# Norm factors and rows of maxima spread over the partitions by DMA through a scratch in memory, instead of by transposes on TensorE

## The chip, the cores and the metric

The kernel runs on one core of one Trainium2 chip. The metric is the device time of one execution in microseconds: 1445.86 us before the change (median of three runs, 1445.59 to 1446.18). All arithmetic is in float32; the large products are made of three TensorE products of numbers split into a high and a low part.

## The reference

The input x has 512 positions of 1024 features. Three blocks work on it one after the other:

```
block 1:  h = rms(x, norm_w) @ w_in                       # 1024 -> 3584 columns
          qa, ka = rms over 64 features of each (head, half), 4 heads x 2 halves
          oa = rms over 128 of (softmax(q0 k0) - lam * softmax(q1 k1)) @ va, per head
          orr = rms over 128 of retention (forward + backward), 4 heads
          x += [oa * silu(ga), orr * silu(gr)] @ w_out
block 2:  mLSTM, 4 heads: gates i, f in both directions; b = cumsum(log_sigmoid(f));
          M = running maximum of (i - b);  weights exp(i - b - M) * (q k), summed over keys,
          divided by max(|sum|, exp(-m));  rms over 256, * sigmoid gate;  x += .. @ m_out
          x += swiglu(rms(x))
block 3:  windowed attention with rope and a sink;  x += .. @ a_out;  x += swiglu(rms(x))
          return rms(x)
```

Two things in it matter here. The rms of queries, keys and head outputs gives one factor for each position (and for each half of a head). The running maximum M of mLSTM is one row of 512 numbers for each head and direction. The kernel keeps features on partitions and positions along the free axis, so each of these rows must be present on all partitions before it can be multiplied or added.

## The kernel before, in words

All activations lie as tiles of 128 features by 512 positions. A weight chunk is 128 x 2048 numbers (1 MB). It is loaded by SyncE's queue into one of two buffers RAW (`w_load`, L352), split by ScalarE into a high part WH and by VectorE into a low part WL (`split`, L299, with `copy`, whose instruction is recorded at L216, and `tt`, L229), and used by TensorE in 48 matmuls: 8 k-tiles, 2 output tiles, 3 products each (`mm3`, L268, recorded at L261). The load of chunk j+2 is put into SyncE's queue when the last part of chunk j has been given to the splitting engines.

The order of the instructions on every engine is written by a planner while the program is built. Each engine has a `Queue` with a model time `t`; each result has a model time in `WHEN`. `weave` (L124) takes pieces of two streams: the main stream (projections, then the output projection) and the side stream (attention, retention or mLSTM heads), and a list `soon` of short steps that are issued when the inputs are due by the model. If the side stream's next piece is due at TensorE's model time it goes first; else the main stream goes on. A stream that finds its input not made gives up its turn. Every engine executes its queue strictly in the planned order and waits on semaphores, so an instruction whose input is late holds all that stands behind it on that engine.

Four pools of buffers are handed out oldest first: 8 banks of PSUM (`bank`), 25 tiles of split operands (`fr`), 12 temporary tiles of 128 x 512 (`ft`), and small columns (`sc`).

Block 1 projects 14 chunks in the order a0 a1 q0 g0 q1 g1 q2 q3 v0 v1 r0 r1 g2 g3. Each q chunk gives a query tile and a key tile of one head. For both, `qk_norm1` copies and squares the tile, `qk_norm2` sums the squares over 64 features with four small matmuls on TensorE (the result is a column of 8 numbers on each of the 128 partitions, one for each of 4 groups of positions and 2 halves), takes the power -1/2 on GpSimd (`rpow`) and multiplies with the block's own norm factor. It then widens the 8 columns to 128 x 512 on VectorE (L754), and `qk_norm3` transposes this with four transposes of 128 x 128 (`spread`, L474, recorded at L293) into a bank of PSUM, from where VectorE multiplies it into the tile. The side stream `diff_heads` works on head hd as soon as the query and key of that head are split; there are 16 items of head and query tile.

The outputs of the heads go through `head_norm`, `head_col` (four small matmuls, a power) and `head_spread` (four transposes, one product on VectorE). Heads 0 to 3 are those of the attention (head 3 is finished in the next side stream, `ret_heads`), 4 to 7 those of the retention. `ret_heads` begins when the four tiles of chunks r0 and r1 are split.

In block 2 `m_gates` computes the gates of all heads with scans on VectorE. The negated maxima NM lie as rows 0 to 3 (forward) and 32 to 35 (backward) of a tile of 64 x 512. Four transposes bring them into 256 columns `ncol`; eight more do the same for two other quantities, `acol` and `ecol`, which the change leaves. For each head, `rows` makes two tiles of 128 x 512 from `ncol` with four transposes and a copy by ScalarE each (L1442 to L1444). `part` then adds a column to such a tile, takes the exponential and multiplies with the product of query and key; the four parts of a head are put into the queues right behind `rows`, without a wait of the planner for the rows. `outp` multiplies with the values. Head hd can start when the main stream has projected its query and key.

`load` (L308) is the helper for single DMAs. The rope step of block 3 (`halves`, L1631) already moves tiles of 32 x 512 from SBUF to SBUF with four DMAs each, which is the only such use before.

Of the kernel before, what the change touches and what calls it, by code (L numbers as in the profile page):

```python
# [5 lines left out]
ALU = mybir.AluOpType  # L6
ACT = mybir.ActivationFunctionType
F32 = mybir.dt.float32
# [4 lines left out]
S = 512  # L13
# [35 lines left out]
WHEN = {}  # L49
# [112 lines left out]
def blocks_kernel(nc, A, out):  # L162
# [64 lines left out]
    def tt(o, a, b, op, *after, q=DV):  # L227
        us = dve_us(o) if q is DV else 0.95
        return q.op(lambda e: e.tensor_tensor(o, a, b, op), *after, us=us)  # L229
# [494 lines left out]

    GS2 = CO[:, K_GS:K_GS + 2]

    def qk_norm1(b, t):

        f, ff = ft.take()
        q, qf = ft.take()  # L730
        t1 = copy(FT[:, f, :], PS[:, b, :], t, ff)
        t2 = act(FT[:, q, :], PS[:, b, :], ACT.Square, t, qf)
        bank.put(b, t1, t2)
        return f, t1, q, t2

    def qk_norm2(got, w):
        f, t1, q, t2 = got
        b, fb = bank.take()
        for i in range(4):
            t = mm(PS[:, b, 2 * i:2 * i + 2], FT[:, q, i * 128:(i + 1) * 128], GS2, True, True, t2, fb, t_co, last=(i == 3))  # L740
        ft.put(q, t)
        m, e, p = sc(8), sc(8), sc(8)
        n, nf = ft.take()
        r2 = ready["r2"][0].unsqueeze(2).to_broadcast([128, 4, 2])
        rc = st["rc"].unsqueeze(2).to_broadcast([128, 4, 2])
        v = lambda x: x.rearrange("p (i g) -> p i g", g=2)
        t = tt(v(m), v(PS[:, b, 0:8]), r2, ALU.mult, t, ready["r2"][1])
        bank.put(b, t)
        t = ts(e, m, EPS, ALU.add, t)
        t = rpow(p, e, 8, t)  # L750

        wide = lambda x: x.unsqueeze(3).to_broadcast([128, 4, 2, 64])
        t = tt(v(m), v(p), rc, ALU.mult, t, st["rct"])
        t = DV.op(lambda e: e.tensor_copy(FT[:, n, :].rearrange("p (i g d) -> p i g d", i=4, g=2), wide(v(m))), t, nf)  # L754
        return f, t1, n, t, w

    def qk_norm3(x):
        f, t1, n, t, w = x
        b, fb = bank.take()
        t = spread(b, lambda i: FT[:, n, i * 128:(i + 1) * 128], t, fb)  # L760
        ft.put(n, t)
        t = stt(FT[:, f, :], FT[:, f, :], w[0], PS[:, b, :], ALU.mult, ALU.mult, t, t1, w[1])
        bank.put(b, t)
        fh, f1 = fr.take()
        fl, f2 = fr.take()
        tk = split(FT[:, f, :], FR[:, fh, :], FR[:, fl, :], t, f1, f2)
        ft.put(f, tk)
        return fh, fl, tk
# [173 lines left out]
    def head_col(x):  # L942

        q, t2, t1, g = x
        b, fb = bank.take()
        for i in range(4):
            t = mm(PS[:, b, i:i + 1], FT[:, q, i * 128:(i + 1) * 128], ONE[:, 0:1], True, True, t2, fb, t_one, last=(i == 3))
        ft.put(q, t)
        m, p = sc(4), sc(4)
        t = ts(m, PS[:, b, 0:4], 1.0 / 128, ALU.mult, t, s2=EPS, op1=ALU.add)  # L950
        bank.put(b, t)
        return p, rpow(p, m, 4, t), t1, g, None

    def head_spread(x):
        p, t, t1, g, _ = x
        b, fb = bank.take()
        t = spread(b, lambda i: p[:, i:i + 1].to_broadcast([128, 128]), t, fb)
        t = tt(G[:, g, :], G[:, g, :], PS[:, b, :], ALU.mult, t, t1)
        bank.put(b, t)
        ready["mix", g] = t  # L960
# [258 lines left out]
    def last_pair(hid):  # L1219
# [64 lines left out]
        r1 = spread_out(1, *sums(1))  # L1284
        store(1, r1, (0, 4), (4, 6), (6, 8))

    def m_gates():

        while "mgate" not in ready:
            yield None  # L1290
        b, tp = ready.pop("mgate")
        T = [ft.take() for _ in range(8)]
        F = [FT[:, x[0], :] for x in T]
        fr_ = [x[1] for x in T]
        t = tt(F[0], PS[:, b, :], RB[:, :], ALU.mult, tp, st["rbt"], fr_)
        st["rb_read"] = t
        bank.put(b, t)
        t = ts(F[0], F[0], SM[:, C_BG:C_BG + 1], ALU.add, t, t_sm)
        yield [t]
        tl = yield from log_sigmoid(F[7], F[0], F[1:7], t, fr_)  # L1300
        yield [tl]

        ones = ONE[64:96, 0:1].to_broadcast([32, S])
        ones2 = ONE[96:128, 0:1].to_broadcast([32, S])
        B, Aa, M, NM, m = F[1], F[2], F[3], F[4], F[5]
        ta = DV.op(lambda e: e.tensor_tensor_scan(B[0:32, :], ones, F[7][64:96, :], 0.0, ALU.mult, ALU.add), tl, t_one, us=1.14)
        yield [ta]
        tb = DV.op(lambda e: e.tensor_tensor_scan(B[32:64, ::-1], ones2, F[7][96:128, ::-1], 0.0, ALU.mult, ALU.add), tl, t_one, us=1.14)
        yield [tb]
        t = tt(Aa[0:64, :], F[0][0:64, :], B[0:64, :], ALU.subtract, ta, tb)  # L1310
        ta = DV.op(lambda e: e.tensor_tensor_scan(M[0:32, :], Aa[0:32, :], Aa[0:32, :], 0.0, ALU.max, ALU.max), t, us=1.14)
        yield [ta]
        tb = DV.op(lambda e: e.tensor_tensor_scan(M[32:64, ::-1], Aa[32:64, ::-1], Aa[32:64, ::-1], 0.0, ALU.max, ALU.max), t, us=1.14)
        yield [tb]
        t1 = ts(NM[0:64, :], M[0:64, :], -1.0, ALU.mult, ta, tb)
        t2 = tt(m[0:64, :], B[0:64, :], M[0:64, :], ALU.add, ta, tb)
        t2 = act(m[0:64, :], m[0:64, :], ACT.Exp, t2, scale=-1.0)
        acol, ecol = sc(256), sc(256)
        yield [t1, t2]
        ncol = sc(256)  # L1320
        b2, f2 = bank.take()
        for i in range(4):
            c = slice(i * 128, i * 128 + 128)
            t3 = tr(PS[:, b2, i * 64:i * 64 + 64], NM[0:64, c], CO[0:64, K_ID:K_ID + 64], t1, f2, t_co, last=(i == 3))
        tc = DV.op(lambda e: e.tensor_copy(ncol, PS[:, b2, 0:256]), t3)
        bank.put(b2, tc)
        b1, f1 = bank.take()
        for i in range(4):
            c = slice(i * 128, i * 128 + 128)
            tr(PS[:, b1, i * 64:i * 64 + 64], Aa[0:64, c], CO[0:64, K_ID:K_ID + 64], t, f1, t_co, last=False)  # L1330
        for i in range(4):
            c = slice(i * 128, i * 128 + 128)
            t3 = tr(PS[:, b1, 256 + i * 64:256 + i * 64 + 64], m[0:64, c], CO[0:64, K_ID:K_ID + 64], t2, last=(i == 3))
        ta = DV.op(lambda e: e.tensor_copy(acol, PS[:, b1, 0:256]), t3)
        tb = DV.op(lambda e: e.tensor_copy(ecol, PS[:, b1, 256:512]), t3)
        bank.put(b1, ta, tb)
        for i in range(8):
            ft.put(T[i][0], t, t1, t3, tl, ta)
        ready["mg"] = (acol, ecol, [ta, tb], ncol, tc)

    def m_proj():
        j, h, l, wt = w_use()
# [86 lines left out]

    def m_heads():  # L1430
        yield from m_gates()
        acol, ecol, tcol, ncol, tnm = ready["mg"]
        V = VF[:, :].rearrange("p (s i n) -> p s i n", s=4, i=4)
        H = {}

        def rows(hd):

            nmb = []
            for d in range(2):
                b, fb = bank.take()  # L1440
                n = 32 * d + hd
                t = spread(b, lambda i: ncol[:, 64 * i + n:64 * i + n + 1].to_broadcast([128, 128]), tnm, fb)  # L1442
                f, ff = ft.take()
                t = copy(FT[:, f, :], PS[:, b, :], t, ff)  # L1444
                bank.put(b, t)
                nmb.append((f, t))
            H[hd] = {"nmb": nmb, "gt": {}, "gtok": {}, "nmr": [[], []]}

# [77 lines left out]
        for hd in range(4):  # L1526
            while ("m", hd) not in ready:
                yield None
            while len(fr.q) < 5:
                yield None  # L1530
            st["fr_kept"] = 5
            rows(hd)
            for i in range(4):
                yield [ready["mqk", hd, 0][2], ready["mqk", hd, 1][2]]
                part(hd, i)
                if i == 1 and o2 is not None:
                    yield from m_turn(*o2)
                    o2 = norm(*o1)
                if i == 3 and o2 is not None:
                    yield from m_turn(*o2)  # L1540
                    o1 = o2 = None
            while ("mv", hd) not in ready:
                yield None
            for i in range(4):
                g = H[hd]["gtok"]
                yield [g[d, kt][1] for d in range(2) for kt in (range(0, i + 1) if d == 0 else range(i, 4))]
                n1 = outp(hd, i)
                n2 = norm(*o1) if o1 is not None else None
                if o2 is not None:
                    yield from m_turn(*o2)  # L1550
                o1, o2 = n1, n2
# [445 lines left out]
```

How the kernel before makes its waits and increments, by code:

```python
    def play(self, eng, sems):  # L92
        for need, fn, inc in self.items:
            for k, v in need:
                eng.wait_ge(sems[k], v)
            ins = fn(eng)
            if inc:
                ins.then_inc(sems[inc[0]], inc[1])
# [1768 lines left out]
        @block.sync  # L1867
        def _(e):
            SP.play(e, sems)
            e.wait_ge(sems["out"], 16 * 6)
```

## Time and profile before

| | |
|---|---|
| median of three runs | 1445.86 us (1445.59 to 1446.18) |
| the profiled execution's own time | 1445.97 us |
| its span, first to last instruction | 1444.2 us |
| granted TensorE clock, mean over the span | 0.999 of full speed |
| TensorE busy | 1431.7 us, 6942 matmuls |
| VectorE busy | 786.5 us |
| ScalarE busy | 583.4 us |
| GpSimd busy | 53.6 us |
| DMA moved | 125.77 MB, mean 87 GB/s |

The span is some 1.8 us shorter than the time of the same execution. A busy figure says in how much of the span the engine had an instruction in work. Matmuls are pipelined: one of 512 columns is recorded with 0.39 us, while the next starts 0.23 us after it. So what a matmul or a transpose costs TensorE is read from the difference of two starts and not from its duration. In the program's names FT is a temporary tile, FR a split operand, SC a column, PS a bank of PSUM, CO the constants (with the identity for transposes), RAW the loaded weights, SPq SyncE's queue of DMAs.

### The profile page before, as it was taken

The numbers are of one execution on the slowest core, as the hardware profiler recorded it, in microseconds if no ns is written. First come the engines' busy times: TensorE is split into PE (matmuls) and PEld (weight loads), VectorE is DVE, ScalarE is ACT, GpSimd is POOL, SyncE is SP. The second block draws the span as 40 slices with busy tenths as digits, with TensorE's granted clock in tenths as the row PEclk, the third lists the DMA queues.
The fourth block names the chain that finished last, engine by engine and source line by source line (L and its number), as shares of the span: only waits on it lengthen the run. The fifth ranks groups of instructions, "written<-read, shape, count | busy, mean of one in ns | idle before, by whom it ended". The sixth has DMA issues, their size and how long they took to land.

```text
span 1444.2 us, 17825 instructions
## 1 busy us (share of the span) xinstructions
PE 1431.7 (99%) x6942; PEld 1164.8 (81%) x6942; DVE 786.5 (54%) x1532; ACT 583.4 (40%) x1091; POOL 53.6 (4%) x108
## 2 busy tenths in 40 slices
PE   9999999999999999999999999999999999999998
PEld 8777767888888888888888888876688888888887
DVE  5667664566477664443355444778564443345443
ACT  5665542344445343222233233667643322232223
POOL 0111001000000000000000000001000000000000
PEclk9999999999999999999999999999999999999999
DMA  6212111121211132222322223321032222322222
GB/s 216 99 71 71 58 59 59 61 101 59 88 59 59 59 117 88 90 90 95 120 95 93 86 87 128 94 83 53 22 117 88 88 91 85 130 88 88 91 83 75
DMA packets 24691, 125.77 MB, mean 87 GB/s; under 512 B 3104, under 2 KB 5792, under 8 KB 13600
## 3 DMA queue, kind: packets, MB, share of 16 engines
q1 hardware_dynamic: 24176, 124.37, 25.2%
q8 instruction: 55, 0.90, 0.2%
q10 hardware_dynamic: 432, 0.27, 0.1%
q14 instruction: 28, 0.23, 0.0%
HBM read 119.91 MB, written 2.10 MB: 84 GB/s over the span
## 4 chain that ended last, share of the span: by engine, by line
PE 94%; DVE 3%; ACT 1%; DMA 1%; issue 1%; SPq 0%; POOL 0%; DVEq 0%; ACTq 0%
PE PS L261 86%; PE PS L284 5%; PE PS L293 3%; DMA RAW<-in_w_in 1%; DVE WL L229 0%; SPq L310 0%; ACT FT L216 0%; DVE ACC L229 0%; DVE FT L234 0%; DVE FT L238 0%; DVE FT L229 0%; DVE G L229 0%; POOL SC L229 0%; DVE FP L238 0%; DVE SC L235 0%
## 5 line engine op out<-in xcount | busy, mean ns | idle before, releaser
L261 PE MATMUL PS<-XH,WH 128*128 128x512 f32 x1080 | 428.4, 397 | 0.0
L261 PE MATMUL PS<-XH,WL 128*128 128x512 f32 x1080 | 420.8, 390 | 0.0
L261 PE MATMUL PS<-XL,WH 128*128 128x512 f32 x1080 | 420.6, 389 | 0.0
L229 DVE TENSOR_TENSOR WL<-RAW,WH 128x512 fp32r<-128x512 f32 (+3 forms) x336 | 273.7, 854 | 130.3 <-ACT WH L216 128.6
L261 PE MATMUL PS<-FR,WH 128*128 128x512 f32 (+1 forms) x1132 | 340.5, 384 | 2.1 <-DVE FR L229 1.5
L216 ACT ACTIVATE WH<-RAW 128x512 fp32r<-128x512 f32 (+3 forms) x336 | 237.6, 755 | 159.0 <-PE PS L261 153.4
L261 PEld LDWEIGHTS PS<-FR,WH 128*128 128x128 f32 x1132 | 207.7, 188 | 44.5 <-ACT FR L216 2.3
L261 PEld LDWEIGHTS PS<-XH,WH 128*128 128x128 f32 x1080 | 202.8, 188 | 46.5 <-issue 5.8
L261 PEld LDWEIGHTS PS<-XH,WL 128*128 128x128 f32 x1080 | 202.7, 188 | 43.0
L261 PEld LDWEIGHTS PS<-XL,WH 128*128 128x128 f32 x1080 | 202.9, 188 | 41.5 <-issue 1.2
L261 PE MATMUL PS<-FR,WL 128*128 128x512 f32 (+1 forms) x566 | 215.8, 381 | 0.0
L229 DVE TENSOR_TENSOR FT<-PS,RB 128x512 f32<-128x512 f32 x89 | 61.0, 687 | 208.3 <-PE PS L261 195.3
L216 ACT ACTIVATE FR<-FT 128x512 fp32r<-128x512 f32 x70 | 44.2, 632 | 280.4 <-DVE FT L229 230.7
L261 PEld LDWEIGHTS PS<-FR,WL 128*128 128x128 f32 x566 | 106.4, 188 | 20.6
L216 ACT ACTIVATE FT<-FT 128x512 f32<-128x512 f32 (+2 forms) x81 | 40.9, 504 | 122.3 <-DVE FT L229 101.6
L229 POOL TENSOR_TENSOR SC<-SC,MH 128x1 f32<-128x1 f32 (+3 forms) x39 | 38.0, 976 | 1273.6 <-DVE SC L235 1046.4
L229 DVE TENSOR_TENSOR FR<-FT,FR 128x512 fp32r<-128x512 f32 x70 | 48.4, 691 | 48.0 <-ACT FR L216 48.0
L229 DVE TENSOR_TENSOR XT<-XT,PS 128x512 f32<-128x512 f32 (+1 forms) x58 | 38.7, 667 | 64.4 <-PE PS L261 64.1
L261 PE MATMUL PS<-WH,XH 128*128 128x512 f32 (+1 forms) x192 | 65.9, 343 | 0.1
L261 PE MATMUL PS<-WH,XL 128*128 128x512 f32 (+1 forms) x192 | 64.6, 337 | 0.0
L261 PE MATMUL PS<-WL,XH 128*128 128x512 f32 (+1 forms) x192 | 64.6, 336 | 0.0
L216 ACT ACTIVATE FT<-XT 128x512 f32<-128x512 f32 (+1 forms) x44 | 26.3, 610 | 83.7 <-DVE XT L229 83.7
(115 smaller groups left out, 1221.7 us busy)
## 6 DMA issues: line engine op xcount, KB each, us to landing
RAW<-in_f_in SPq DMA_DIRECT2D x44, 1024.0 KB, 4.8
RAW<-in_w_in SPq DMA_DIRECT2D x12, 1024.0 KB, 4.8
RAW<-in_m_in SPq DMA_DIRECT2D x12, 1024.0 KB, 4.8
RAW<-in_f_oa SPq DMA_DIRECT2D x16, 768.0 KB, 4.1
RAW<-in_f_ob SPq DMA_DIRECT2D x16, 640.0 KB, 3.8
RAW<-in_a_in SPq DMA_DIRECT2D x6, 1024.0 KB, 4.9
RAW<-in_w_out SPq DMA_DIRECT2D x4, 1024.0 KB, 4.9
RAW<-in_m_out SPq DMA_DIRECT2D x4, 1024.0 KB, 4.8
```

The source lines that it names most:

```text
L216: return AC.op(lambda e: e.activation(o, i, f, scale=scale) if accum is None else e.activation(o, i, f, scale=scale, accum_out=accum), *af ...
L229: return q.op(lambda e: e.tensor_tensor(o, a, b, op), *after, us=us)
L261: f = lambda e: e.matmul(o, l, r, start=start, stop=stop, skip_group_check=True)
L284: f = lambda e: e.matmul(o, l, r, start=start, stop=stop, skip_group_check=True)
L293: f = lambda e: e.transpose(o, i, ident)
```

## The change

The transposes for eight query and key tiles, for the heads 0, 1 and 2 and for the maxima of mLSTM go away. In their place the columns are written to a tensor in memory in such an order that they form a row, and the row is read back into all 128 partitions. SyncE issues these DMAs and waits for the first before it issues the second. The result is in an FT tile and not in a bank of PSUM. The helper gives the planner 4.0 us for the write and 3.0 us for the read, beside 0.45 us for each issue.

```
+    SCR = nc.dram_tensor("scr", (16, 2 * S), F32, kind="Internal").ap()
+    used = [0]
+
+    def spread_by_dma(cols, groups, f, tok, free):
+
+        k, g = used[0], groups
+        used[0] += 1
+        row = SCR[k:k + 1, 0:g * S]
+        s = dsem(f"sc{k}")
+        dst = row.rearrange("o (j p) -> p (o j)", p=128)
+        SP.add(lambda e: e.dma_start(dst, cols, allow_slow_non_contiguous=True), [tok], (s, 16), 0.45)
+        WHEN[s, 16] = SP.t + 4.0
+        t = (s, 16)
+        s = dsem(f"sb{k}")
+        SP.t = max(SP.t, due(t))
+        for m in range(g):
+            o, i = slice(128 // g * m, 128 // g * (m + 1)), row[:, S * m:S * m + S].to_broadcast([128 // g, S])
+            SP.add(lambda e, o=o, i=i: e.dma_start(FT[o, f, :], i), [t, free], (s, 16), 0.45)
+        WHEN[s, 16 * g] = SP.t + 3.0
+        return (s, 16 * g)
 
     qk_norm2:
-        wide = lambda x: x.unsqueeze(3).to_broadcast([128, 4, 2, 64])
-        t = tt(v(m), v(p), rc, ALU.mult, t, st["rct"])
-        t = DV.op(lambda e: e.tensor_copy(FT[:, n, :].rearrange("p (i g d) -> p i g d", i=4, g=2), wide(v(m))), t, nf)
-        return f, t1, n, t, w
+        t = tt(m.rearrange("p (g i) -> p i g", g=2), v(p), rc, ALU.mult, t, st["rct"])
+        return f, t1, n, spread_by_dma(m, 2, n, t, nf), w
 
     qk_norm3:
-        b, fb = bank.take()
-        t = spread(b, lambda i: FT[:, n, i * 128:(i + 1) * 128], t, fb)
+        t = stt(FT[:, f, :], FT[:, f, :], w[0], FT[:, n, :], ALU.mult, ALU.mult, t, t1, w[1])
         ft.put(n, t)
-        t = stt(FT[:, f, :], FT[:, f, :], w[0], PS[:, b, :], ALU.mult, ALU.mult, t, t1, w[1])
-        bank.put(b, t)
 
     head_col:
-        return p, rpow(p, m, 4, t), t1, g, None
+        t = rpow(p, m, 4, t)
+        if g in BY_DMA:
+            n, nf = ft.take()
+            return p, spread_by_dma(p, 1, n, t, nf), t1, g, n
+        return p, t, t1, g, None
+
+    BY_DMA = (0, 1, 2)
 
     head_spread:
-        p, t, t1, g, _ = x
+        p, t, t1, g, n = x
+        if n is not None:
+            ready["mix", g] = t = tt(G[:, g, :], G[:, g, :], FT[:, n, :], ALU.mult, t, t1)
+            ft.put(n, t)
+            return
 
+    ROWS = nc.dram_tensor("rows", (64, S), F32, kind="Internal").ap()
     m_gates:
-        ncol = sc(256)
-        b2, f2 = bank.take()
-        for i in range(4):
-            c = slice(i * 128, i * 128 + 128)
-            t3 = tr(PS[:, b2, i * 64:i * 64 + 64], NM[0:64, c], CO[0:64, K_ID:K_ID + 64], t1, f2, t_co, last=(i == 3))
-        tc = DV.op(lambda e: e.tensor_copy(ncol, PS[:, b2, 0:256]), t3)
-        bank.put(b2, tc)
...
         for i in range(8):
-            ft.put(T[i][0], t, t1, t3, tl, ta)
-        ready["mg"] = (acol, ecol, [ta, tb], ncol, tc)
+            if i != 4:
+                ft.put(T[i][0], t, t1, t3, tl, ta)
+        ready["mg"] = (acol, ecol, [ta, tb], None, load(ROWS, FT[0:64, T[4][0], :], "rows", t1))
+        ft.put(T[4][0], ready["mg"][4])
 
     rows(hd) in m_heads:
-                b, fb = bank.take()
                 n = 32 * d + hd
-                t = spread(b, lambda i: ncol[:, 64 * i + n:64 * i + n + 1].to_broadcast([128, 128]), tnm, fb)
                 f, ff = ft.take()
-                t = copy(FT[:, f, :], PS[:, b, :], t, ff)
-                bank.put(b, t)
+                t = load(FT[:, f, :], ROWS[n:n + 1, :].to_broadcast([128, S]), f"nm{n}", tnm, ff)
                 nmb.append((f, t))
 
     the loop over the heads in m_heads:
-            rows(hd)
+            if hd == 0:
+                rows(0)
             for i in range(4):
                 yield [ready["mqk", hd, 0][2], ready["mqk", hd, 1][2]]
                 part(hd, i)
...
+            if hd < 3:
+                rows(hd + 1)
             while ("mv", hd) not in ready:
                 yield None
```

The last edit also moves the rows of heads 1, 2 and 3: they are issued after the parts of the head before, and not at the start of their own head.

## Rows read from the trace of the kernel before

**Rows 1.** The page, parts 1 and 4: busy time; shares of the chain by engine.
```profile
PE 1431.7 (99%) x6942; PEld 1164.8 (81%) x6942; DVE 786.5 (54%) x1532; ACT 583.4 (40%) x1091; POOL 53.6 (4%) x108
...
PE 94%; DVE 3%; ACT 1%; DMA 1%; issue 1%; SPq 0%; POOL 0%; DVEq 0%; ACTq 0%
```

**Rows 2.** Windows: PE, PEld, DVE, ACT, POOL busy (instructions), clock, DMA share, GB/s.
```profile
60.00:240.00 180.00, 180.00 (x869) 132.29 (x869) 113.28 (x270) 92.75 (x181) 16.58 (x12) 1.00 0.17 59
...
320.00:460.00 140.00, 139.87 (x694) 118.53 (x694) 92.14 (x238) 63.87 (x140) 6.26 (x11) 1.00 0.20 68
```

**Rows 3.** Waits of PE: waiting line and releaser, us in total, times, longest.
```profile
PE PS L293 <- DVE FT L754: 0.5, 1, 0.5
```

**Rows 4.** Timeline around one query tile's spread: start us, duration us, instruction.
```profile
45.72 0.39 PE L261 MATMUL PS<-XH,WL 128*128 128x512 f32 x1
...
45.95 0.60 PE L293 MATMUL PS<-CO,FT 128*128 128x128 f32 x4
...
46.31 0.47 PE L261 MATMUL PS<-XH,WH 128*128 128x512 f32 x1
...
46.62 0.39 PE L261 MATMUL PS<-XL,WH 128*128 128x512 f32 x1
```

**Rows 5.** Timeline of PE, head 0's spread and what follows it.
```profile
120.95 0.65 PE L293 MATMUL PS<-CO,SC 128*128 128x128 f32 x4
121.44 0.60 PE L293 MATMUL PS<-CO,FT 128*128 128x128 f32 x4
```

**Rows 6.** Timeline of PE, mLSTM: columns, rows of head 0, parts of head 0.
```profile
332.54 0.96 PE L293 MATMUL PS<-CO,FT 64*128 64x64 f32 x12
333.52 1.09 PE L293 MATMUL PS<-CO,SC 128*128 128x128 f32 x8
334.36 2.98 PE L261 MATMUL PS<-FR 128*128 128x512 f32 x12
```

**Rows 7.** DMA queues and issues: tensors, count, KB each, us to landing.
```profile
q1 hardware_dynamic: 24176, 124.37, 25.2%
...
RAW<-in_w_in SPq DMA_DIRECT2D x12, 1024.0 KB, 4.8
...
FT<-FT SPq DMA_DIRECT2D x40, 64.0 KB, 2.0
...
out<-G SPq DMA_DIRECT2D x4, 256.0 KB, 2.6
...
FT<-in_pos SPq DMA_DIRECT2D x1, 256.0 KB, 5.1
...
SM<-in_small ACTq DMA_DIRECT2D x1, 4.0 KB, 2.9
```

**Rows 8.** Timeline: power, product and widening of the first query tile.
```profile
43.51 1.64 POOL L229 TENSOR_TENSOR SC<-SC,MH 128x8 f32<-128x8 f32 x1 [16.35 <-DVE SC L234]
...
45.19 0.17 DVE L229 TENSOR_TENSOR SC<-SC 128x8 f32<-128x8 f32 x1 [1.75 <-POOL SC L229]
...
45.39 0.43 DVE L754 COPY FT<-SC 128x512 f32<-128x512 f32 x1
```

**Rows 9.** Timeline: a weight load's issue and the next chunk's first split.
```profile
117.43 0.33 SPq L357 DMA_DIRECT2D RAW<-in_w_in  x1
...
130.88 1.14 ACT L216 ACTIVATE WH<-RAW 128x512 fp32r<-128x512 f32 x2
```

**Rows 10.** Timeline of PE: first scores, last head sums of attention, first retention products.
```profile
54.66 1.66 PE L261 MATMUL PS<-FR 64*128 64x512 f32 x12
...
173.83 0.70 PE L261 MATMUL PS<-ONE,FT 128*128 128x1 f32 x5
...
194.97 1.20 PE L261 MATMUL PS<-FR 64*128 64x512 f32 x8
```

**Rows 11.** The chain in order of time (start us, us): projections in mLSTM.
```profile
334.60 10.89 PE PS L261 x48
...
352.03 33.35 PE PS L261 x147
```

More of the change, by code:

```diff
@@ L1431, in m_heads @@
         yield from m_gates()
-        acol, ecol, tcol, ncol, tnm = ready["mg"]
+        acol, ecol, tcol, _, tnm = ready["mg"]
         V = VF[:, :].rearrange("p (s i n) -> p s i n", s=4, i=4)
```

## The prediction

> **What bounds the kernel now.** I read the page first, then windows of each stage, then the waits of TensorE (PE), then timelines around each edit. The page shows PE busy for 1431.7 of 1444.2 us, and 94% of the chain that ended last is PE's [rows 1]. That is a mean, so the windows decide: in block 1's woven part PE is busy for 180.00 of 180 us, in mLSTM's for 139.87 of 140 [rows 2]. VectorE (DVE) stands at 113 of 180 and 92 of 140 there, ScalarE (ACT) lower, the DMA engines at 0.17 and 0.20. So in both stages that the change touches each PE slot is time, and the other engines have room. The reader is to see in the waits that PE hardly waits for what is removed: one wait of 0.5 us for the widened columns [rows 3].
>
> The sum is made against the profiled execution's 1445.97 us (span 1444.2 and some 1.8 around it), 0.1 above the median of 1445.86.
>
> **What goes from PE.** The cost of four transposes is read from starts.
> - Query and key tiles, 8 spreads. The transposes start at 45.95, the next matmul at 46.31, and its successor 0.31 us later where 0.23 is the rule: 0.36 + 0.08 = 0.44 us [rows 4]. 8 x 0.44 = 3.5 us.
> - Heads 0, 1, 2. From 120.95 to 121.44: 0.49 us [rows 5], for three 1.4 us (0.06 off for where they touch other transposes, as taken).
> - mLSTM's rows: eight transposes, two tiles, from 333.52 to 334.36: 0.84 us [rows 6]. Four heads, 0.8 each: 3.2 us.
> - Columns of maxima: 4 of the 12 transposes from 332.54 to 333.52: 0.33 us [rows 6].
> - The wait of 0.5 us [rows 3].
>
> Together 80 instructions and 3.5 + 1.4 + 3.2 + 0.3 + 0.5 = 8.9 us. Also gone are eight wideners on DVE (0.43 us each [rows 8]), one small copy, and eight copies by ACT. Neither engine is the bound; I count them as nothing, bounds 0 and 1 us of gain at the end of mLSTM, where head 3's rows stand before its parts.
>
> **What comes: the two DMAs, and what they hold.** The trace has no DMA of single numbers. The write moves 1024 numbers of 4 bytes (512 for a head) to places 4 bytes wide, since neighbours in a column block go to places 128 numbers apart. Below it is bounded by 2.0 us, the landing of FT<-FT [rows 7]. Above: the queue's mean packet takes 0.252 x 1444.2 x 16 / 24176 = 0.24 us; 64 packets on each of 16 engines are 15 us, on top of 2.0 that is 17 us. The nearest row is the load of 4 KB in 128 rows, 2.9 us [rows 7], with 8 pieces for each engine and not 64. I take 4.4 us, from that row: 56 more pieces on each engine at a tenth of the mean packet (0.027 us, they carry next to nothing) add 1.5. The read of a row into 128 partitions (256 KB) lies between 2.6 us (256 KB stored) and 5.1 us (256 KB loaded) [rows 7]; I take 3.4.
>
> The Trainium skill's page "DMA: Bandwidth & Descriptors", section "Rules for kernel authors", says that a transfer whose last dimension isn't contiguous becomes one descriptor for each element, and advises against it. That is the one rule that speaks against this change: it makes 1024 pieces of one write, as I counted, and it says nothing of their price, so by it the write may lie anywhere up to my upper bound; the first rival is what it would do. The same page's fit for a single DMA ("Anatomy of one DMA", 2.0 us and bytes over 436 GB/s) would make the write an estimated 2.0 us and the read 2.6; then no engine would wait and the sum would be the bare 8.9. The row of 2.9 us for 4 KB stands above that fit.
>
> Chain of a tile, from the product's end at 45.4 us [rows 8]: before, widening and transposes until about 46.5. After: issue 0.45, write 4.4, two issues 0.8, read 3.4, so about 9 us, 8 us later. Who waits for that?
> - *The side stream of block 1.* The key's DMAs queue behind the query's on SyncE, so the first scores move from 54.66 [rows 10] to about 62. The main stream, a projection, fills PE meanwhile. The heads' own spreads cost the side stream its DMA time where the next step came sooner: some 2.5 us for head 1, 5 for head 2, none for head 0 (by the same timeline its spread stood 22 us behind its sums). Together 13 to 16 us late at the end of the attention. Its last sums are at 173.8, and the retention waits for its projections until 194.97 [rows 10]: 21 us of cover. Without it the delay would show in full, less the output projection on heads 0 to 3: 2 chunks x 4 k-tiles x 2 x 3 = 48 matmuls at 0.23, 11 us.
> - *SyncE's queue.* It stands some 4.5 us in each write, and before that for the power (1.64 us) and product. Behind it stand weight loads. The tightest load is issued at 117.43, lands 4.8 us later and is first split at 130.88 [rows 7, 9]: 8.6 us of room for a delay of 2 to 5 us. Nothing.
> - *DVE.* The multiplication by the row is placed by the planner when it is due by the model (0.45 + 4.0, then 0.9 + 3.0 = 8.35 us for a tile, 7.9 for a head). My 9 us is 0.7 above this for a tile. In 11 places DVE, in order, stands for what is late, and behind it weight splits and softmax steps. The splits are made a chunk ahead; the softmax steps reach PE through its transposes. Of some 0.7 us each, 8 us in all, I let PE see an eighth: 1.0 us (bounds 0 and 8).
> - *mLSTM, head 0.* NM is ready some 4 us ahead of the transposes' end at 334.36 [rows 6]; store (2.9, as for a small transfer), read (3.4) and issues make the rows come 3 to 5 us later than now. The parts are in the queues behind them without a planner's wait, so DVE and ACT stand 3 to 5 us, and with them the splits and value copies. PE has the parts' own 12 matmuls and a value projection, 10.89 us from 334.60 [rows 6, 11]. Covered; then 33.35 us of pure projection [rows 11] let the heads catch up. Price 0, up to 4 if the cover is too short.
> - *Rows of heads 1 to 3* are read a whole `outp` ahead. Nothing is late next.
> - Traffic: 19 rows of 256 KB, 4.9 MB on 125.77, on engines busy for a fifth.
>
> Sum: 8.9 - 1.0 = 7.9 us; 1445.97 - 7.9 = 1438.1, against the median 1438.0. Own range 1435.3 (all 8.9, the idle at mLSTM's end and a luckier order) to 1440.5.
>
> **Rivals.**
> 1. *The scratch is slow, and the kernel slower.* If each of 1024 pieces costs like a small packet of its own, the write lands after 7 us and more. DVE then stands 2.6 us + 0.7 at each of 11 products, the planner having put work behind them; beyond about 1 us of slack each, PE sees it: 11 x 2.3 = 25 us, less 8.9: 1462. With 6.0 us it is 11 x 1.3 = 14, less 8.9: 1451. It decides from 11 x (late - 1) = 8.9, a lateness of 1.8 us, or a write of about 5.5 us. For it: no such DMA in the trace, and an upper bound of 17 us. Against: the 4 KB load with 2.9. Chance 0.17.
> 2. *One cover is too short.* Splits behind DVE's wait in mLSTM (4 us) or a weight load behind SyncE's waits show at PE: 8.9 - 1.0 - 4 = 4 us of gain, 1442. For it: the chunks q2 and q3 follow each other, so four tiles' DMAs come within some 15 us, just ahead of the load of [rows 9]. Against: 8.6 us of room there. Chance 0.13.
> 3. *It frees PE and nothing moves.* The side stream, late by 13 to 16 us and more if reads take 5.1 us (11 x 1.7 = 19 us more), overruns the 21 us of cover, PE idles at the start of retention or the output projection for 6 to 9 us and the gain is given back: 1445. For it: the side's length becomes DMA latency. Against: the heads' waits are mostly in parallel, and the output projection is a second cover. Chance 0.10.
>
> **How the numbers follow.** Forecast 0.60, rivals 0.17, 0.13, 0.10. No change is within 0.2% (2.9 us), about what a measurement can tell: 1443.0 to 1448.8. Faster: 0.60 and nearly all of rival 2, 0.72. Same: rival 3 and edges, 0.12. Slower: 0.16. The range for 8 in 10 reaches from 1435.0 to 1447.0; above it lies most of rival 1.
>
> **What would show it.** Right: matmul records at L293 down by 80, PE still busy for all of the two windows, the side's last attention sums before the retention's first products, writes to the scratch landing in 3 to 5 us, no wait of PE above 1 us that hangs on a DMA. Wrong: DVE waits for the scratch in the list of waits with more than 10 us in total, or PE idle beyond 5 us between 60 and 460 us. A write above 5.5 us makes rival 1; retention products that start at once behind the attention's end make rival 3.

## The result: slower by 2.1%, and the profile after

| | before | after |
|---|---|---|
| median | 1446.02 us (1445.59 to 1446.23, 4 runs) | 1476.69 us (1475.0 to 1478.6, 4 runs) |
| span of the profiled execution | 1444.2 us | 1476.3 us |
| its own time | 1445.97 us | 1478.32 us |
| TensorE busy | 1431.7 us, 6942 matmuls | 1432.4 us, 6862 matmuls |
| mean granted clock | 0.999 | 0.984 |

The ratio is 1.0213 (95%: 1.02 to 1.0225). I had forecast 1438.0 with a range to 1447.0: wrong in sign. The 80 transposes are gone, as forecast. The page's parts 1 and 4, then the windows of block 1's woven part and of mLSTM's (shifted by 35 us), answer to [rows 1, 2]:

```profile
PE 1432.4 (97%) x6862; PEld 1163.3 (79%) x6862; DVE 783.0 (53%) x1523; ACT 572.0 (39%) x1078; POOL 53.6 (4%) x108
...
PE 86%; DMA 7%; DVE 4%; ACT 2%; SPq 1%; issue 1%; POOL 0%; DVEq 0%; ACTq 0%
PE PS L261 80%; DMA scr<-SC 4%; PE PS L284 4%; DMA FT<-scr 2%; PE PS L293 2%; DMA RAW<-in_w_in 1%; DVE FT L238 1%; ACT FT L216 0%; SPq L310 0%; DVE WL L229 0%; DVE FT L234 0%; POOL SC L229 0%; DVE ACC L229 0%; ACT WH L216 0%; DVE FR L229 0%
```

```profile
60.00:240.00 180.00, 148.05 (x678) 109.46 (x677) 96.28 (x244) 76.05 (x158) 14.60 (x10) 0.88 0.25 68
355.00:495.00 140.00, 139.88 (x681) 118.05 (x679) 93.73 (x245) 61.17 (x136) 6.26 (x11) 1.00 0.26 84
```

mLSTM is as full as before; block 1 has 32 us in which TensorE does nothing, and a mean granted clock of 0.88. The transposes of `m_gates` start at 368.35 us; before, they started at 332.54 [rows 6]. So block 1 lost 35.8 us, and what follows won 3.7 (the spans differ by 32.1).

```profile
368.35 0.71 PE L293 MATMUL PS<-CO,FT 64*128 64x64 f32 x8
```

TensorE's own waits name the engine before it, VectorE's and ScalarE's name the DMA (waiting line and releaser, us, times, longest):

```profile
PE PS L261 <- DVE FR L229: 23.7, 5, 17.8
PE PS L261 <- ACT FT L216: 8.3, 3, 5.2
```

```profile
DVE FT L238 <- DMA FT<-scr: 39.1, 6, 14.7
...
ACT FT L218 <- DMA FT<-rows: 10.4, 1, 10.4
...
DVE FT L238 <- DMA FT<-rows: 8.3, 1, 8.3
...
DVE G L229 <- DMA FT<-scr: 3.4, 1, 3.4
```

The DMA issues with their median landing answer to [rows 7]; the last line is that of SyncE's waits:

```profile
FT<-scr SPq DMA_DIRECT2D x16, 128.0 KB, 4.1
FT<-rows SPq DMA_DIRECT2D x8, 256.0 KB, 4.8
...
scr<-SC SPq DMA_DIRECT2D x8, 4.0 KB, 9.5
rows<-FT SPq DMA_DIRECT2D x1, 128.0 KB, 6.0
scr<-SC SPq DMA_DIRECT2D x3, 2.0 KB, 8.3
```

```profile
SPq L744 <- DMA scr<-SC: 102.8, 11, 13.8
```

A write of 4 KB lands after 9.5 us, where the planner was told 4.0 and I took 4.4. The timeline of SyncE's queue shows the standing, with a DMA packet count of the first write's stretch (45.5 to 55.5 us, 40 slices) below it:

```profile
45.06 0.38 SPq L737 DMA_DIRECT2D scr<-SC  x1
55.89 1.17 SPq L744 DMA_DIRECT2D FT<-scr  x2
57.11 0.59 SPq L737 DMA_DIRECT2D scr<-SC  x1
...
141.80 0.42 SPq L737 DMA_DIRECT2D scr<-SC  x1
156.10 1.10 SPq L744 DMA_DIRECT2D FT<-scr  x2
157.29 0.54 SPq L357 DMA_DIRECT2D RAW<-in_w_in  x1
157.88 0.42 SPq L737 DMA_DIRECT2D scr<-SC  x1
171.24 1.09 SPq L744 DMA_DIRECT2D FT<-scr  x2
```

```profile
DMA  0077300000000000000000000000000000000000
...
DMA packets 1040, 0.00 MB, mean 0 GB/s; under 512 B 1040, under 2 KB 1040, under 8 KB 1040
```

The reader is to see two things. In this first write, with nothing else under way, the 1024 pieces pass the DMA engines in under 1 us and are done by 47 us; then the engines are idle for 8 us while SyncE waits for the completion. And the writes issued at 141.80 and 157.88, each right behind a weight load of 1 MB (the first of these loads at 141.37), take 14.3 and 13.4 us. For the first of the two the packets themselves run late. The DMA engines' busy tenths in 40 slices from 141.8 to 156.1 us show it: the engines are at work until some 150 us, and what is left is completion.

```profile
DMA  0000039799999999998752100000000000000000
```

The long writes end in the largest hole, on VectorE and then on TensorE:

```profile
180.68 0.75 DVE L238 SCALAR_TENSOR_TENSOR FT<-FT,SM 128x512 f32<-128x512 f32 x1 [14.70 <-DMA FT<-scr]
```

```profile
182.95 1.65 PE L261 MATMUL PS<-FR 64*128 64x512 f32 x6 [17.81 <-DVE FR L229]
184.53 0.79 PE L261 MATMUL PS<-WH,XH 128*128 128x512 f32 x1
185.12 0.63 PE L261 MATMUL PS<-WL,XH 128*128 128x512 f32 x1
185.55 0.63 PE L261 MATMUL PS<-WH,XL 128*128 128x512 f32 x1
```

From the first of these holes on, TensorE works for a time at a granted clock of 0.50 (1.2 GHz): in the rows above matmuls start 0.43 us apart instead of 0.23. TensorE's holes over 1 us in block 1 are of 2.96, 4.41, 1.59, 5.18 and 17.81 us and end at 64.39, 73.02, 105.39, 132.87 and 182.95. The windows of its work behind the first, second, fourth and fifth show the clock (the third number from the end, ahead of DMA share and GB/s):

```profile
64.90:68.60 3.70, 3.70 (x11) 2.60 (x11) 0.00 (x0) 0.00 (x0) 0.00 (x0) 0.50 0.33 19
73.00:78.50 5.50, 5.48 (x21) 4.03 (x22) 3.65 (x15) 3.12 (x8) 1.63 (x1) 0.50 0.38 121
132.90:139.90 7.00, 7.00 (x21) 5.84 (x22) 4.32 (x10) 2.10 (x4) 1.64 (x1) 0.50 0.04 0
183.00:187.70 4.70, 4.70 (x14) 3.28 (x15) 3.33 (x10) 1.03 (x4) 0.00 (x0) 0.50 0.23 54
```

That is 20.9 us of work at half clock. At 0.43 instead of 0.23 us for each matmul it gives away an estimated 9.7 us. Idle time and clock less what the change took from TensorE in block 1 (3.5 + 1.4 + 0.5) make 32 + 9.7 - 5.4 = 36.3 us, against 35.8 measured.

### The profile page after: what moved, and what is told of

The parts are those of the page before. It is cut to its first block, busy times and chain, and to the rows that moved or that the text cites. A ratio compares the mean times of both kernels' runs of the same rounds, so it can differ in the third digit from the quotient of the medians.

```text
span 1476.3 us, 17695 instructions
## 1 busy us (share of the span) xinstructions
PE 1432.4 (97%) x6862; PEld 1163.3 (79%) x6862; DVE 783.0 (53%) x1523; ACT 572.0 (39%) x1078; POOL 53.6 (4%) x108
## 4 chain that ended last, share of the span: by engine, by line
PE 86%; DMA 7%; DVE 4%; ACT 2%; SPq 1%; issue 1%; POOL 0%; DVEq 0%; ACTq 0%
PE PS L261 80%; DMA scr<-SC 4%; PE PS L284 4%; DMA FT<-scr 2%; PE PS L293 2%; DMA RAW<-in_w_in 1%; DVE FT L238 1%; ACT FT L216 0%; SPq L310 0%; DVE WL L229 0%; DVE FT L234 0%; POOL SC L229 0%; DVE ACC L229 0%; ACT WH L216 0%; DVE FR L229 0%
## 5 line engine op out<-in xcount | busy, mean ns | idle before, releaser
L261 PE MATMUL PS<-FR 64*128 64x512 f32 (+3 forms) x384 | 59.9, 392 | 25.0 <-DVE FR L229 22.2
L261 PEld LDWEIGHTS PS<-FR 64*128 64x128 f32 (+1 forms) x384 | 36.3, 194 | 40.3 <-DVE FR L229 23.4
```

The lines of the kernel that those rows point to most:

```text
L261: f = lambda e: e.matmul(o, l, r, start=start, stop=stop, skip_group_check=True)
```

## The experiments

Medians are against 1445.8 to 1446.2 us of the kernel before, run on the same chip.

**Which part.** Three kernels make one part of the change each, by putting the lines of before back for the others.

> Only mLSTM's rows of maxima go through memory (one store of 64 rows of 2 KB, eight reads); queries, keys and heads 0 to 2 keep their transposes. Theory A (the loss is made by the slow write of single numbers to the scratch, 9.5 us against the 4.0 that the planner was told, and only block 1 has it): this part gains what it takes from PE, 32 + 4 transposes or 3.5 us, since it has no such write: 1442.5 (1441.5 to 1443.5). Theory B (any round trip through memory costs, since DVE stood 8.3 us for the rows of head 0 and traffic grows): 1446 or more.

Measured: 1442.36 us, ratio 0.9975 (0.9965 to 0.9984): 3.6 us gained, against 3.5 forecast. VectorE stood 7.2 and ScalarE 9.3 us for head 0's rows, and it cost nothing that shows: the cover that the prediction named held.

> Only the eight query and key tiles go through the scratch; heads and mLSTM's rows as before. Theory A (slow writes, and the waits of PE of 2.96, 4.41, 1.59, 5.18 and 17.81 us all hang on query or key tiles): nearly the whole loss is here: 1446 - 4 + 35, less a few us because three head writes no longer stand in SyncE's queue: 1472 to 1480. Theory C (the queue of SyncE is what overflows, eleven writes of 9 us within 170 us, and each tile's write waits for those ahead): taking the three head writes out frees 30 us of the queue, and the time drops clearly: 1455 to 1465.

Measured: 1467.74 us, ratio 1.0155: 21.7 us lost. Less than theory A said, more than C.

> Only heads 0, 1 and 2 go through the scratch. Both theories A and C: the side stream is given the DMA's time for each, 13 us instead of 8, but it has 21 us of room before the retention: 1446 - 1.4 = 1444.6 (1443.5 to 1446.5). If DVE's stand at the products reaches PE here too (3.4 us was seen at one head), 1447 to 1450.

Measured: 1451.78 us, ratio 1.004 (1.0025 to 1.0055): 5.8 us lost, above both. SyncE's timeline of this kernel, then TensorE's, show how:

```profile
105.52 0.38 SPq L737 DMA_DIRECT2D scr<-SC  x1
116.78 0.33 SPq L744 DMA_DIRECT2D FT<-scr  x1
117.20 0.86 SPq L357 DMA_DIRECT2D RAW<-in_w_in  x2
```

```profile
128.69 1.11 PE L293 MATMUL PS<-CO,FT 128*128 128x128 f32 x4 [5.34 <-DVE FT L775]
```

One head's write held SyncE from 105.52 to 116.78. The weight load behind it, issued at 105.32 in the kernel before, went out at 117.20 and landed 7.3 us later, at 124.50. ScalarE stood 5.8 us for it, and behind that stood a step of a query tile for which TensorE waited 5.34 us. In the kernel before the first split of that load, on ScalarE, started at 118.59:

```profile
118.59 0.61 ACT L216 ACTIVATE WH<-RAW 128x512 fp32r<-128x512 f32 x1
```

Behind the hole TensorE's clock was at 0.50 for 3.1 us more (window of this kernel):

```profile
128.70:131.80 3.10, 3.10 (x10) 2.62 (x11) 3.00 (x10) 1.92 (x5) 0.00 (x0) 0.50 0.00 0
```

That is the prediction's second rival. The parts sum to -3.6 + 21.7 + 5.8 = 23.9 us; the whole change has 30.7. So 6.8 us appear only with all parts together. The longest write took 11.6 us and TensorE's longest hole 5.0 us in the kernel with queries and keys alone, 14.3 and 17.8 in the whole change; no run separates what makes them longer.

**The write.** The next kernels change only how the numbers go to memory.

```
e4:  dst = row.rearrange("o (p j) -> p (o j)", p=128)
e7:  dst = row.rearrange("o (p j) -> p (o j)", p=128)[:, ::-1]
e13: dst = row.rearrange("o (p j h) -> p (o j) h", p=128, h=2)[:, ::-1, :]
e9:  for j in range(4 * g): dma_start(dst[:, j:j + 1], cols[:, j:j + 1])      # dst as in the change
e15: dma_start(mid[:, ::-1], cols)     # SBUF to SBUF, then mid to memory as in e4
```

> All of the change, but each write to the scratch lays the numbers down as they lie in SBUF, 128 pieces of 32 (or 16) bytes instead of 1024 (or 512) pieces of 4 bytes; the factors then come to the wrong positions, all other work is the same. Theory A (the number of pieces makes the write slow, and the slow write makes the loss): the write lands after some 3 us, within the planner's 4.0, and the forecast's sum comes true: 1437 to 1441. Theory C (SyncE's queue standing for completions, whatever their length, holds weight loads and the next tile): the write is 3 us but queueing stays: 1450 or more. If the write is slow because its target is memory and not because of the pieces, it still lands after 8 to 9 us and the time stays at 1476.

> All of the change, but each partition's 8 (or 4) numbers are written in reverse order into 32 (or 16) bytes of their own. So there are 1024 (or 512) pieces of 4 bytes as in the change, but no two partitions write within the same 32 bytes; the factors come to wrong positions, all other work is the same. If the number of pieces makes the write slow: landing at 8 to 10 us again and 1470 to 1480. If it is that 16 DMA engines write 4 bytes each into the same lines of memory: landing within 3 us and about 1436, as with the contiguous write.

> All of the change; the write has 512 (256) pieces of 8 bytes, pairs in reverse order within each partition's own 32 (16) bytes; the factors come to wrong positions, all other work is the same. If only pieces of 4 bytes complete late: landing within 3 us and a time of 1436 to 1440. If it is any reordering into pieces below 16 bytes: 7 to 10 us and 1465 to 1477.

> All of the change; each write of 1024 (512) pieces of 4 bytes is issued as 8 (4) DMAs of 128 pieces of 4 bytes, one column each, with the same places in memory and the factors right. In the trace of the change the pieces themselves are through the DMA engines within 0.7 us, and the completion comes 8 to 10 us later, nearly the same for 512 pieces as for 1024. If a DMA with many pieces is what completes late: each DMA completes in 2 to 3 us, the whole write in 5 to 6, inside the plan, and the time is 1437 to 1440. If a write of 4-byte pieces completes late however few they are: 8 to 10 us again or more, 1475 or above.

> All of the change, with one DMA more in each chain: the numbers are first written from SBUF to SBUF in reverse order within each partition, in 1024 (512) pieces of 4 bytes, and from there to memory as in the contiguous kernel, in 128 pieces of 32 (16) bytes; the factors come to wrong positions, all other work is the same. If it is memory as the target that completes 4-byte pieces late: the first DMA lands in 2 to 2.5 us, the chain is some 2 us longer than in the contiguous kernel, and the time is 1436 to 1442. If pieces of 4 bytes are slow wherever they go: 7 to 10 us and 1465 to 1480.

| kernel | pieces of a tile's write | median landing | time |
|---|---|---|---|
| the change | 1024 x 4 bytes | 9.5 us | 1476.69 |
| e7 | 1024 x 4 bytes, each partition's in 32 bytes of its own | 9.6 us | 1468.54 |
| e9 | 8 DMAs of 128 x 4 bytes, all under way together | 7.5 us each | 1467.89 |
| e13 | 512 x 8 bytes | 4.3 us | 1436.19 |
| e4 | 128 x 32 bytes | 1.7 us | 1436.18 |
| e15 | 1024 x 4 bytes to SBUF, then as e4 | 2.5 us, then 1.4 | 1437.06 |

Rows of the DMA issues: the contiguous kernel's, then e13's, e9's and e15's.

```profile
scr<-SC SPq DMA_DIRECT2D x8, 4.0 KB, 1.7
```

```profile
scr<-SC SPq DMA_DIRECT2D x8, 4.0 KB, 4.3
```

```profile
scr<-SC SPq DMA_DIRECT2D x76, 0.5 KB, 7.5
```

```profile
SC<-SC SPq DMA_DIRECT2D x8, 4.0 KB, 2.5
scr<-SC SPq DMA_DIRECT2D x8, 4.0 KB, 1.4
```

Contiguous pieces of 32 bytes land within the plan and the loss is gone (e4). Sharing of lines by several engines is not the main cause (in e7 a tile's write lands no faster), nor are pieces of 4 bytes as such (e15): what is slow is 4-byte pieces with memory as the target. Whether their number adds to it, e9 doesn't settle, since its eight DMAs are under way together. The first DMA of each write, 128 pieces with none of its own kind ahead, landed after 4.2 to 8.1 us (median 5.8), the last after 7.9 to 10.0. Here are the fastest first DMAs of a tile and of a head, at 88.3 and 153.5 us:

```profile
L738 SPq DMA_DIRECT2D scr<-SC x1: 583/583/583, 88.3 to 88.3; - x1
...
DMA to landing us min/median/max: 4.5/4.5/4.5
```

```profile
DMA to landing us min/median/max: 4.2/4.2/4.2
```

That is three times the 1.4 us in which a head's 128 contiguous pieces land in e4, so the size counts even with 128 pieces. Their number may add to it; no run has 128 of them alone. Two results lie outside what was expected: e7 came out 1.5 us below its range, 8 us below the change with the same landing for tiles (6.9 us instead of 8.3 for heads), and e9 with 7.5 us landed between its two cases and was 7 us faster than the second. Neither difference is explained; in e9 the seven more issues of a tile also tell the planner 3.2 us more of the chain.

With the long write gone, the whole change gains 9.8 us (e4: ratio 0.9932, 0.9917 to 0.9947), a little more than the bare 8.9 of the sum. e13 lies between in landing, 4.3 us, and has no loss, which fits with the 4.0 that the planner was told. Theory A holds; theory C, that queueing on SyncE would remain with a short write, falls.

**The planner's numbers.** Does the long write harm in itself, or because the order was made for a short one?

```
-        WHEN[s, 16] = SP.t + 4.0            ->  + 9.7
-        WHEN[s, 16 * g] = SP.t + 3.0        ->  + 4.2
-NFT = 12                                    ->  13
```

> The kernel with queries and keys alone through the scratch (1467.74 us), but the planner is told 9.7 us for the write and 4.2 for the read, as measured, instead of 4.0 and 3.0; with one more temporary tile (13), since tiles are held longer in its plan. The 4-byte pieces are as before. Theory D (the write's length does harm because the planner did not know it: products stood at the head of VectorE's queue and scores at the head of TensorE's): the planner puts other work there, VectorE no longer waits for the scratch and the time falls to 1445 to 1452. Theory C (SyncE's queue is held 14 us for each tile whatever the plan says, eight tiles in a row, and weight loads come late): VectorE's waits go, but TensorE still idles by 15 to 20 us in sum, 1460 or more.

Measured: 1445.18 us (1444.23 to 1450.73, 10 runs), ratio 1.0003 (0.9993 to 1.0014). The write landed even later, after 12.2 us, and VectorE no longer waited for the scratch.

> Control for e5_told_the_truth: queries and keys through the scratch with the planner's old times (4.0 and 3.0) and 13 temporary tiles instead of 12. If the true times made the gain of 22.6 us there (theory D): as with 12 tiles, 1465 to 1471. If the thirteenth tile made it: 1445 to 1450.

Measured: 1468.24 us. So the thirteenth tile does nothing with the old numbers, and the step from here to e5, which changes the two numbers alone, is worth 23 us. This is theory D: an engine in order stood at the head of its queue. Whether the true numbers would do as much with 12 tiles, no run shows.

> As e5_told_the_truth (with 12 tiles), and the two reads of a tile are put into SyncE's queue only when the write is due by the plan, so that weight loads and the next tile's write go ahead of them and SyncE hardly stands for a write. Theory C: this is what was missing, 1442 to 1446, at least 10 us below the kernel that is only told the times. Theory D: SyncE's standing had cover, so no more than 3 us below it. If the side stream's late start and end are the bound (latency itself), both stay above 1450.

Measured: 1452.06 us, 6.9 above e5. The gain that theory C promised didn't come; reads and writes then stand behind weight loads (128 KB read in 7.0 us instead of 3.4). But this kernel has 12 temporary tiles and e5 has 13, so two things differ, and how the 6.9 us divide between them is open. It has 22 more of the filler matmuls that the planner puts where it foresees idle time (L256: 84, 62 in e5, 52 before), and a missing tile could make such time too.

> The whole change with 9.7 and 4.2 us told to the planner and 13 temporary tiles; pieces of 4 bytes as before. Theory D: 1445.2 for queries and keys, less 3.6 for mLSTM's rows, and 0 to 6 for the heads: 1441 to 1448. Theory C (eleven long writes overflow SyncE's queue, and the three head writes come between weight loads): 1450 or more.

Measured: 1470.93 us: true numbers alone don't mend the whole change. By its time alone this is theory C's case; the next kernel tells that theory from the side stream's wait. The planner itself saw idle time: it placed 160 fillers, against 78 in the next kernel, e14. And VectorE still stood at two of the heads' products, 23.0 us in all; behind the longer stand (the last line below) TensorE had its longest hole, 7.5 us. The fillers of e11, then of e14, then a row of VectorE in e11:

```profile
L256 PE MATMUL PS<-ONE x160: 270/275/421, 109.2 to 1462.8; 128*128 128x128 f32 x160
```

```profile
L256 PE MATMUL PS<-ONE x78: 271/275/377, 110.1 to 1435.5; 128*128 128x128 f32 x78
```

```profile
239.47 0.69 DVE L229 TENSOR_TENSOR G<-G,FT 128x512 f32<-128x512 f32 x1 [13.96 <-DMA FT<-scr]
```

The next kernel's edit, in short:

```
     head_spread(x), called by the side stream behind `yield` of the power alone:
+            t = spread_by_dma(p, 1, n, t, nf)
+            def product(): ready["mix", g] = x = tt(G[:, g, :], G[:, g, :], FT[:, n, :], ALU.mult, t, t1); ...
+            soon.append((t, product))
```

> As e11_all_told_the_truth (the planner told 9.7 and 4.2 us, 13 temporary tiles, 1470.93 us), but the product of heads 0 to 2 is placed when its row is due, and the side stream goes on without waiting for it. Theory E (rival 3 of the prediction: the side stream, made to wait some 15 us for each of three heads, is what brought that kernel 25 us above the one with queries and keys alone; its planner filled 108 more idle slots): 1442 to 1447, and the filler matmuls back from 160 to under 70. If the heads' writes harm by standing in SyncE's queue before weight loads: 1455 or more still.

Measured: 1443.84 us (1441.58 to 1452.16, 10 runs), ratio 0.9991 (0.9977 to 1.0006). So with a write of 11.6 us, making the side stream wait for three heads' rows costs 27 us against placing their products when they are due, and without that wait the change is no loss, and no measurable gain. The 27 us hold both the plan's idle time and VectorE's stands at the products, which are gone too. The first of the two is the third rival's mechanism, larger than I had it. In the change itself it doesn't show: with 4.0 us told the planner placed the 52 fillers of the kernel before, and VectorE stood instead.

**A version that beats both.**

```
e8, e12:  t = tr(PS[0:c, b, 0:128], m, IDN, tok, fb, t_co)        # c = 8 (4): one transpose, rows of 128
          t = DV.op(lambda e: e.tensor_copy(FT[0:c, y, 0:128], PS[0:c, b, 0:128]), t, yf, us=0.2)
          t = load(row.rearrange("o (j p) -> (o j) p", p=128), FT[0:c, y, 0:128], f"sc{k}", t)
e16:      stationary FT[:, q, i:512:4]; dst = row.rearrange("o (g p i) -> p (o g) i", p=128, i=4)
e17:      act(FT[:, q, :].rearrange("p (i c) -> p c i", i=4), PS[:, b, :].rearrange("p (c i) -> p c i", i=4), Square)
```

> mLSTM's rows through memory as in the change; heads by transposes as before; queries and keys: one transpose of 128 x 8 on TensorE makes 8 rows of 128, VectorE copies them to SBUF, the write has 8 pieces of 512 bytes, and the read is that of the change. Against the mLSTM-only kernel (1442.36) TensorE loses eight times four transposes less one (0.44 - 0.19 us each) and the wait of 0.5: 2.5 us, so 1440 (1439 to 1441.5) if a write of few pieces lands in 2 us. If a small write to memory is slow whatever its pieces, 1455 or more.

Measured: 1438.39 us, ratio 0.9947 (0.9932 to 0.9962), 0.6 us below the expected range.

> As e8_row_by_one_transpose, and the heads 0 to 2 in the same way: one transpose of 128 x 4, a write of 4 pieces of 512 bytes, a read; the product is placed when its row is due and the side stream doesn't wait for it. TensorE loses three times 0.49 - 0.19: 1438.4 - 0.9 = 1437.5 (1437 to 1438.5). If SyncE's standing for these writes delays a weight load as in the heads-only kernel: 1439 to 1442.

Measured: 1437.69 us, ratio 0.9943 (0.9926 to 0.9959): the best kernel here with all factors at their places, 8.4 us below the kernel before and 39 below the change.

> All of the change, and the factors right, with a write of 16-byte pieces: the small matmuls that sum the squares take every fourth position as their columns (i, i + 4, ...), so that partition p holds the factors of positions 4p to 4p + 3, which lie side by side in the row. The block's own norm factors are computed once more in that order (four small matmuls, 0.5 us). If the contiguous kernel's 1436.18 holds with 0.5 for these: 1436.7 (1436.0 to 1437.5). If a stationary operand with a step of 16 bytes loads more slowly, some 60 small matmuls at 0.1 us more: 1440 or more.

Measured: 1450.04 us, ratio 1.0028: the write landed in 2.4 us, but TensorE paid. Timeline of e16:

```profile
43.11 1.80 PE L261 MATMUL PS<-CO,FT 128*128 128x2 f32 x8
44.77 0.47 PE L261 MATMUL PS<-XH,WH 128*128 128x512 f32 x1
```

Eight small matmuls take 1.66 us; in the kernel before, such a group at 42.08 was followed at 42.89.

> As e16_strided_columns, but the reordering is done where the squares are written: ScalarE writes the squares of every fourth position side by side, and TensorE's small matmuls read 128 columns without a step (only the four for the block's own factors keep the step of 16 bytes). In e16 eight small matmuls with the step took 1.66 us from the first to the next group, in the kernel before 0.81; 11 groups of 0.85 are 9.4 us, and the own factors about 1.7 more. If this step is the whole difference to the contiguous kernel (1436.18): 1436.2 + 1.7 = 1437.9 (1437 to 1439), if ScalarE's write with a step of 512 bytes costs nothing to the path. If that write is slow and the tile's chain grows: 1440 or more.

Measured: 1439.34 us, ratio 0.9954 (0.9938 to 0.9971). Most of e16's loss is gone, so the step was its main cause; 1.4 us above the 1437.9 expected are not accounted for.

## Why the prediction was wrong

1. *What bounds the kernel.* Right: TensorE in both woven parts.
2. *What goes from TensorE, 8.9 us.* Right, slightly small: 9.8 in the kernel with the contiguous write, 3.6 for mLSTM's part against 3.5. Where the 0.9 above the sum comes from is not traced.
3. *The write, "I take 4.4 us, from that row: 56 more pieces on each engine at a tenth of the mean packet".* This is the step that failed. It measured 9.5 us (8.3 for a head; 8.0 to 14.3 over all). I scaled a row with pieces of 32 bytes that goes to SBUF to pieces of 4 bytes that go to memory. The pieces' own time was indeed short, under 1 us in the first write; the late part is the completion, which no row of before showed for such a DMA. My bounds were 2 and 17 us and I took a value near the lower one. The read was off too, by less: 4.1 us for a tile and 5.9 for a head, where I took 3.4. The step from there to the price failed with it: I let VectorE stand 0.7 us at each product and TensorE see 1.0 us in all; VectorE stood 42.5 us and TensorE 32.
4. *The first rival.* It named this mechanism and its point of decision, 5.5 us. At 9.5 us its own formula gives 11 x (5.1 + 0.7 - 1) = 53 us less 8.9, so 1490; measured 1476.7. The lateness was not paid at 11 places but at a few: VectorE stood 39.1 us at 6 tiles and 3.4 at one head, and TensorE 32 us in all, with the half clock on top. I gave it 0.17. Only 3.5 of the 15 us between my bounds lay below the 5.5 us that decide, so its chance should have been far larger.
5. *The Trainium skill's rule* ("DMA: Bandwidth & Descriptors", "Rules for kernel authors": a non-contiguous last dimension becomes one descriptor for each element, so rearrange) speaks against the change and the trace agrees: 1040 packets. Following it (e4, e12) is what makes the gain. But the number of descriptors alone is not the price: e15 has the same 1024, with SBUF as the target, and lands in 2.5 us. The fit that the prediction takes from the same page of the Trainium skill ("Anatomy of one DMA") is stated there for DMAs issued by GpSimd, and the DMAs here are SyncE's. Its estimates were 2.0 us for the write and 2.6 for the read; measured were 9.5, and 4.1 (a tile) and 5.9 (a head).
6. *SyncE's queue, "8.6 us of room ... Nothing".* Wrong with the real write: I took a delay of 2 to 5 us. In the heads-only kernel one weight load went out 12 us late and cost TensorE 5.3 us (rival 2, though at another load than I had named). The rows were also read wrongly: the split at 130.88 belongs to the load issued at 105.32, whose first split is at 118.59, and not to that of 117.43. ScalarE splits a chunk in four steps, here at 118.59, 119.45 and two from 130.88 on, and in the heads-only kernel the late load held up the first of them. The load of 105.32 is the tight one; it landed at 110.1 and had 8.5 us of room, so that my 8.6 came out nearly right by luck.
7. *DVE's wait in mLSTM, price 0.* The price was right: in the mLSTM-only kernel no time was lost. The stand was not: 8.3 and 10.4 us in the change where I had 3 to 5, since the store took 6.0 us and not 2.9, the reads 4.8 and not 3.4.
8. *The side stream's 21 us of cover.* The delay was larger than forecast, but the cover held in the change. The first scores came at 73.02 us, where I had about 62. The attention's last sums and the retention's first products are these rows of the change:

```profile
222.99 0.95 PE L261 MATMUL PS<-ONE,FT 128*128 128x1 f32 x8
...
230.78 2.35 PE L261 MATMUL PS<-FR 64*128 64x512 f32 x18
```

So some 7 of the 21 us were left. With true numbers told (e11) the side stream's wait did cost time, as the 27 us of e14 show.
9. *Not foreseen:* the clock. TensorE stood still for 3.0 to 17.8 us at a time, and behind four such holes it worked 20.9 us at 1.2 GHz instead of 2.4, an estimated 9.7 us of the loss.

## What to carry to other kernels

In this kernel a transpose moved from TensorE to a DMA paid only where the pieces that go to memory were not single 4-byte numbers: look in the trace at the time from the issue to the landing and not at the packets. In a program whose order is planned, put the measured latency into the plan before judging the change, and let nothing but the consumer wait: with all three parts in, slow writes cost 30.7 us with the plan misinformed, 24.8 with true latencies, and nothing that can be measured once the side stream no longer waited (e14, whose runs spread over 10 us). A queue that waits for its own DMA holds the loads behind it, and so a cost appears at an engine that never touches the scratch.

## What the runs showed of the hardware

- A write to memory in 4-byte pieces landed after a median of 9.5 us with 1024 pieces (8.0 to 14.3) and 8.3 with 512 (6.9 in e7); with 128 pieces in each of eight DMAs under way together after 7.5 (4.2 to 10.0). 512 pieces of 8 bytes took 4.3 us, 128 of 32 bytes 1.7. In the first write of the change the packets' records end within 1 us and the landing comes some 9 us later; behind a weight load the packets run late too. What happens between packets and landing no trace shows.
- The same 4-byte pieces from SBUF to SBUF land in 2.5 us (e15).
- Eight small float32 matmuls with a stationary operand read at a step of 16 bytes take 1.66 us instead of 0.81 (e16).
- A row of 2 KB read from memory into 128 partitions (256 KB in one DMA) lands after a median of 3.0 us (e12) to 5.9 us (the change).
- In the change TensorE's granted clock was 0.50 behind holes of 2.96, 4.41, 5.18 and 17.81 us, over 3.7, 5.5, 7.0 and 4.7 us of work; in the heads-only kernel over 3.1 us behind one of 5.34.
